# Modulation rows in column tiles of TensorE: four tiles for the early rows, two for the late ones, with the late bias on VectorE

## The chip, the cores and the metric

The kernel runs on one core of one Trainium2 chip. A core has TensorE (PE, which multiplies matrices; its weight loads are listed as PEld), VectorE (DVE), ScalarE (ACT), GpSimd (POOL) and SyncE (SP, which here only issues transfers). TensorE writes its results into PSUM banks of 128 partitions by 512 fp32 values. The metric is the device time of one execution in microseconds (us), lower is better. Everything is fp32, and each fp32 multiplication shows in the trace as two passes (two MATMUL records, each with a weight load).

## The reference

One layer of a diffusion backbone on 128 context tokens and 1024 latent tokens with 1024 channels. What matters here is its beginning:

```
mod = silu(cvec) @ ada_w + ada_b                # 1024 -> 6144, for c_ctx and for c
sh1, sc1, gt1, sh2, sc2, gt2 = split(mod, 6)
h = rms_norm(x, norm1) * (1 + sc1) + sh1
p = h @ w_in                                    # 1024 -> 2432
... token mixing (scans and pooling), output projection with gt1,
... a mixture of 16 experts with sh2, sc2, gt2, final norm
```

The modulation has two rows of 6144 values, one for the context's vector `c_ctx`, one for the latent's `c`. `sh1` and `sc1` (the first 2048 columns) are needed before the projection `h @ w_in` can begin; the other 4096 are needed only after the token mixing.

## The kernel before

The phases run one after the other: projection (`project_phase`, 0 to about 407 us), scans, output projection, experts, final norm. The change touches `project_phase` only, and the parameter table that the host packs.

**Orders.** Each engine has its own program, written out by hand in the function under `@block.<engine>`; semaphores order them (`wait_ge`). The order of work within an engine is therefore fixed, and a waiting instruction holds all that stand behind it.

**Modulation.** The 6144 columns are made in 12 rows of 512 columns (`NADA`), each for both vectors. A row of `ada_w` (1024 x 512, 2 MB) comes in two halves of 1 MB into `ada`, a buffer that holds one row. SyncE's `load_ada(j)` issues half `h` once the semaphore `ada_used` says that the same half of row j-1 has been used, and then the bias `ada_b` (2 KB, on one partition).

- *Early rows*, j = 0 to 3 (`NEARLY` = 4): TensorE's `modulate(j)` multiplies, for each of the eight groups of 128 channels, `silu_c` (128 x 2) with the 128 x 512 weights, all into partitions 0 and 1 of `ps_row`, and adds the bias by a multiplication with `ones` on one partition (L512, L514). ScalarE's `take_row` copies the 2 x 512 result to `mod_row` (L329). TensorE's `turn_row` transposes it in four pieces into `ps_mod` (L530). After row 3, VectorE copies `ps_mod` to `mod` (L439) and derives `g1`.
- *Late rows*, i = 0 to 7: VectorE's `modulate(i)` (L485, L487) multiplies and adds the weights by the channels' factors, sixteen operations of 128 x 512 for each row (eight for each vector), into `mod_sum`. TensorE's `add_up(i)` then adds up the 128 partitions with `pick_row` and adds the bias (L523, L524). ScalarE takes the row and sends it to memory (`modrow`).

**Tokens.** x arrives in three groups of three tiles of 128 tokens. ScalarE squares them (L334), VectorE scales them (L434), TensorE transposes them (`turn_x`, L539), and ScalarE copies the result to `hT` (`take_x`, L347). TensorE's order in the early part is: `turn_x(0)`, `modulate(0)`, `turn_x(1)`, `turn_x(2)`, `turn_row(0)`, then `modulate(j)` and `turn_row(j)` for j = 1 to 3. ScalarE's is: all squares, `take_x(0)`, `take_row(0)`, `take_x(1)`, `take_x(2)`, then the rows 1 to 3. When `mod` is there, ScalarE (L373) and VectorE (L447) apply the modulation to `hT`.

**Projection.** 19 projections of 128 output columns (`project(n, b)`, L563: 24 fp32 multiplications, 48 passes with 384 moving columns), in pairs: `pair(i)` is two projections and then `add_up(i - 1)`. Their weights `win` (0.5 MB each) have two buffers. ScalarE copies each result from PSUM to `pad`. The first four projections feed GpSimd's pooling, the other fifteen VectorE's `shift` (L453 to L467). VectorE's loop is: `modulate(i + 1)`, then two shifts. After the pairs come the pooling's four multiplications (L587) and the last projection.

Of the kernel before, what the change touches and what calls it, by code (L numbers as in the profile page):

```python
# [17 lines left out]
ALU = mybir.AluOpType  # L18
ACT = mybir.ActivationFunctionType
# [36 lines left out]
for _name, _k in (("c", 16), ("norm1", 8), ("mu", NZ), ("pool_scale", 4), ("head", 4 * 10)):  # L56
    PCOLS[_name] = (_n, _n + _k)
    _n += _k
# [61 lines left out]
def project_phase(nc, st, io, keep):  # L120
# [6 lines left out]
    ones = cst[0:1, CCOLS["blk"][0]:CCOLS["blk"][0] + 2]  # L127

    hT = keep["wide"][:].rearrange("p (k c) -> p k c", k=KT)
    HK = KT // 2  # L130
    ada = sb("ada", [P, 2, HK, 512])
    ada_b = sb("ada_bias", [1, 512])
    mod_row = sb("mod_row", [2, 512])

    mod_sum = sb("mod_sum", [P, 2, 512])
    pick_row = sb("pick_row", [P, 2, 2])
# [9 lines left out]
    silu_c = sb("silu_c", [P, KT, 2])  # L146
# [73 lines left out]
    def _(eng):  # L220
        def load_ada(j):
            for h in range(2):
                if not isinstance(j, int) or j > 0:
                    eng.wait_ge(ada_used, 2 * j - 1 + h)
                eng.dma_start(ada[:, h], ada_v[h, :, :, ds(j * 512, 512)]).then_inc(ada_in[h], 16)
            if not isinstance(j, int) or j > NEARLY:

                eng.wait_ge(row_ps, j - NEARLY)
            eng.dma_start(ada_b[:], io["ada_b"][ds(j * 512, 512)].unsqueeze(0)).then_inc(ada_in[1], 16)
# [19 lines left out]
        for n in range(2, 4):  # L249
            eng.wait_ge(win_used, n - 1)  # L250
            load_win(n)
        load_ada(NEARLY)
        eng.dma_start(pw[:], io["pool_w"].rearrange("g c d -> c g d")).then_inc(pw_in, 16)

        eng.wait_ge(zero_set, 1)
# [18 lines left out]
    def _(eng):  # L274
# [4 lines left out]
        for s in range(2):  # L279
            for r in range(2):  # L280
                eng.memset(pick_row[:, s, r:r + 1], float(r == s)).then_inc(pick_set, 1)
# [41 lines left out]
    def _(eng):  # L323
        def take_row(j, late=False):
# [4 lines left out]
            eng.activation(mod_row[:], ps_row[0:2], ACT.Copy).then_inc(row_sb, 1)  # L329
# [56 lines left out]
        def pair(i):  # L386
# [9 lines left out]
            eng.dma_start(io["modrow"][:, ds((i - 1) * 512, 512)], mod_row[:]).then_inc(row_out, 16)  # L396
# [22 lines left out]
    def _(eng):  # L419
        ch = Chain(eng, pre_chain)  # L420
        eng.wait_ge(silu_done, 1)
        ch(eng.tensor_tensor(silu_c[:].rearrange("p k s -> p (k s)"), sig_c[:], par[:, 0:16], ALU.mult))
# [3 lines left out]
        for g in range(3):  # L426
# [45 lines left out]
        def modulate(i):  # L472
# [5 lines left out]
            for h in range(2):  # L478
                eng.wait_ge(ada_in[h], (i + NEARLY + 1) * 16 * (h + 1))
# [24 lines left out]
    def _(eng):  # L504
        def modulate(j):

            for h in range(2):
                eng.wait_ge(ada_in[h], 16 * (h + 1) * (j + 1))
# [2044 lines left out]
```

## Time and profile before

| | us |
|---|---|
| median of 3 runs | 3016.3 (3009.99 to 3019.97) |
| the profiled execution | 3018.82 |
| its span, first to last instruction | 3016.4 |
| TensorE busy in the span | 2721.9 (90%) |
| VectorE busy | 1158.6 (38%) |
| ScalarE busy | 577.9 (19%) |
| GpSimd busy | 564.9 (19%) |
| mean granted TensorE clock | 0.956 of full |

The busy times are sums over stages with different limits, so the table alone does not say what an edit in one stage is worth. Times in the rows below count from the start of the span. The granted clock is given as a share of 2.4 GHz; it has two levels in this trace, 1.00 and 0.50, and a figure between is a mean over a stretch.

### The profile page before, as it was taken

The page shows a single profiled execution, that of the slowest core. Times are in us where ns is not written, and L with a number is a line of the kernel's source. Part 1 is how long each engine was busy: PE and PEld are TensorE (multiplying, and loading weights), DVE is VectorE, ACT ScalarE, POOL GpSimd, SP SyncE. Part 2 cuts the span into 40 slices and gives each one's busy share as a digit, 9 for nine tenths or more (in the row PEclk, how much of TensorE's full clock was granted, in tenths as well). Part 3 has the DMA queues.
Part 4 walks back from the last instruction along what each step waited for, and adds up shares of the span by engine and source line. Part 5 has one row for each costly group of instructions (what it writes and reads, how often), then busy time and mean ns, then how long its engine had stood idle before and what let it go on. Part 6 is the DMA issues. An engine that isn't in the chain of part 4 may idle for free. (4 is left out here: it accounts for less than half of the span.)

```text
span 3016.4 us, 75964 instructions
## 1 busy us (share of the span) xinstructions
PE 2721.9 (90%) x33244; PEld 2404.6 (80%) x33244; DVE 1158.6 (38%) x3005; ACT 577.9 (19%) x1471; POOL 564.9 (19%) x571
## 2 busy tenths in 40 slices
PE   7999958887878897967999999999999999999991
PEld 2555527787877883437999999999999999999991
DVE  1388565555564443334213321232223221332125
ACT  4010153343442332320000100011000100010002
POOL 0683024434445331000000000000000000000002
PEclk9999978898999999978999999999999999999996
DMA  5522210000001004017687777777687768777753
GB/s 206 166 98 84 84 40 7 3 4 7 4 6 38 6 5 179 28 50 294 258 315 266 266 265 275 280 282 271 242 317 281 269 243 316 266 266 264 276 210 133
DMA packets 235260, 517.97 MB, mean 172 GB/s; under 512 B 9854, under 2 KB 42878, under 8 KB 234939
## 3 DMA queue, kind: packets, MB, share of 16 engines
q1 hardware_dynamic: 224410, 483.14, 43.8%
q0 software_dynamic: 8176, 21.83, 3.0%
q10 hardware_dynamic: 2480, 10.06, 0.8%
q8 instruction: 166, 2.72, 0.4%
q14 instruction: 28, 0.22, 0.0%
HBM read 488.68 MB, written 26.33 MB: 171 GB/s over the span
## 5 line engine op out<-in xcount | busy, mean ns | idle before, releaser
L2313 PE MATMUL ps_h<-xT,w1c 128*128 128x144 f32 x4096 | 547.3, 287 | 1.3 <-ACT xT L2119 1.3
L2313 PE MATMUL ps_h<-xT,w3c 128*128 128x144 f32 x4096 | 544.4, 287 | 0.0
L2313 PEld LDWEIGHTS ps_h<-xT,w1c 128*128 128x128 f32 x4096 | 520.5, 191 | 1.7 <-ACT xT L2119 1.7
L2313 PEld LDWEIGHTS ps_h<-xT,w3c 128*128 128x128 f32 x4096 | 519.9, 191 | 0.0
L2323 PE MATMUL ps_ye<-he,w2c 128*128 128x144 f32 x4096 | 512.3, 286 | 0.0
L2323 PEld LDWEIGHTS ps_ye<-he,w2c 128*128 128x128 f32 x4096 | 505.9, 191 | 0.0
L2268 DVE TENSOR_TENSOR u<-ps_h,sig 128x144 f32<-128x144 f32 x256 | 78.7, 307 | 888.7 <-ACT sig L2150 888.7
L563 PE MATMUL front_bank<-wide,win 128*128 128x384 f32 x912 | 298.1, 489 | 2.0 <-DVE wide L447 2.0
L2150 ACT ACTIVATE sig<-ps_h 128x144 f32<-128x144 f32 x256 | 74.3, 290 | 1065.9 <-PE ps_h L2313 1065.9
L563 PEld LDWEIGHTS front_bank<-wide,win 128*128 128x128 f32 x912 | 173.8, 191 | 127.3 <-issue 9.2
L2181 POOL DMA_INDIRECT acc<-ys,idx_s x16 | 25.8, 1615 | 1002.8 <-ACT ye_p L2139 872.0
L896 POOL TENSOR_TENSOR lm<-am,cst 128x256 f32<-128x256 f32 x216 | 162.4, 768 | 231.4 <-DVE am L1269 88.4
L1280 DVE TENSOR_TENSOR tw<-bank,tw 128x512 f32<-128x512 f32 x144 | 99.1, 690 | 260.9 <-PE bank L1438 260.8
L1438 PE MATMUL bank<-tw,xw 64*64 64x64 f32 x2880 | 170.8, 223 | 11.0 <-issue 9.5
L1438 PE MATMUL bank<-xw,tw 64*64 64x64 f32 x2304 | 151.7, 226 | 21.7 <-ACT xw L1064 16.3
L1438 PEld LDWEIGHTS bank<-tw,xw 64*64 64x64 f32 x2880 | 154.0, 139 | 18.2 <-issue 14.2
L1438 PEld LDWEIGHTS bank<-xw,tw 64*64 64x64 f32 x2304 | 135.0, 141 | 28.1 <-ACT xw L1064 19.9
L2175 POOL DMA_INDIRECT xs<-h,idx_s x17 | 17.0, 1001 | 706.0 <-DVE idx_p L2238 706.0
L1438 PE MATMUL bank<-tw,lm 64*64 64x64 f32 x2880 | 112.8, 224 | 24.5 <-POOL lm L896 13.7
L1438 PEld LDWEIGHTS bank<-tw,lm 64*64 64x64 f32 x2880 | 104.3, 139 | 31.0 <-issue 16.0
L2219 DVE TENSOR_SCALAR_CACHE_REDUCE after<-prow,pcol 128x128 f32<-128x128 f32 (+2 forms) x153 | 115.5, 755 | 0.1
L487 DVE SCALAR_TENSOR_TENSOR mod_sum<-ada,silu_c,mod_sum 128x512 f32<-128x512 f32 x112 | 104.9, 936 | 5.5 <-DVE mod_sum L487 1.6
(284 smaller groups left out, 3146.1 us busy)
## 6 DMA issues: line engine op xcount, KB each, us to landing
w1c<-in_w SPq DMA_DIRECT2D x64, 2048.0 KB, 8.0
w3c<-in_w SPq DMA_DIRECT2D x64, 2048.0 KB, 13.0
w2c<-in_w SPq DMA_DIRECT2D x64, 2048.0 KB, 13.2
ada<-in_ada_w SPq DMA_DIRECT2D x24, 1024.0 KB, 6.1
prow<-probsT ACTq DMA_DIRECT2D x17, 576.0 KB, 7.1
win<-in_w_in SPq DMA_DIRECT2D x19, 512.0 KB, 3.9
z<-in_x_all SPq DMA_DIRECT2D x3, 1536.0 KB, 13.9
acc<-zero SPq DMA_DIRECT2D x9, 512.0 KB, 7.0
```

What stands on the lines that cost most here:

```text
L487: mc(eng.scalar_tensor_tensor(out, ada[:, h, k], c, out, ALU.mult, ALU.add))
L563: ins = eng.matmul(ps_p[b][c][:, 0:PIECE], win[:, b, k], hT[:, k, c * PIECE:(c + 1) * PIECE], start=(k == 0), stop=(k == KT - 1))
L896: eng.tensor_tensor(lm[:, b, lv % 2].rearrange("p (d h) c -> p d h c", d=2), am[:, n % 4, :, :, 2], lvl[:, :, lv].unsqueeze(2).to_broadcas ...
L1280: ins = eng.tensor_tensor(flat, INV[b][:], flat, ALU.add)
L1438: return eng.matmul(out, a, b, start=start, stop=stop, skip_group_check=True)
L2150: eng.activation(sig[:, f % 2], ps_h[f % 2][:, 0:SLOTS], ACT.Sigmoid).then_inc(sig_done, 1)
L2175: eng.indirect_dma_start(xs[:], None, io["h2"], bass.IndirectOffsetOnAxis(ap=idx_s[:, 0], axis=0)).then_inc(gathered, 16)
L2181: eng.indirect_dma_start(io["acc"], bass.IndirectOffsetOnAxis(ap=idx_s[:, 1], axis=0), ys[:], None, compute_op=ALU.add).then_inc(scattered ...
L2219: eng.tensor_scalar(after[:, 0:hi - me], prow[:, me:hi], p, None, ALU.is_gt, ALU.add, accum_out=cnts[:, t, 1:2])
L2268: eng.tensor_tensor(u[:, f % 2], ps_h[f % 2][:, 0:SLOTS], sig[:, f % 2], ALU.mult).then_inc(u_done, 1)
L2313: ins = eng.matmul(ps_h[g % 2][:, off:off + SLOTS], w[:, b, k, f * P:(f + 1) * P], xT[:, k], start=(k == 0), stop=(k == KT - 1))
L2323: ins = eng.matmul(yps(k), w2c[:, b, f, k * P:(k + 1) * P], he[:, b, f], start=(c == 0 and f == 0 and k % 3 == 0), stop=(c == NCHUNK - 1 a ...
```

## The change

1. `modulate` on TensorE sends the four channel groups of each half to four column tiles: group k writes the partitions 32k to 32k + 31 of `ps_row`. For this `silu_c` is widened from 2 to 32 columns, of which 30 are zero. Groups k and k + 4 are added in the same tile, and four partial sums stand in four groups of partitions. The bias is no longer added here.
2. `take_row` copies all 128 partitions for an early row, 33 for a late one.
3. `turn_row` multiplies `mod_row` (128 x 128 pieces) with `pick` (128 x 2, ones where a partition holds the wanted vector) in place of the four transposes. This turns the row and adds the four partial sums. `pick` is made by VectorE in three additions from the identity matrix.
4. The early bias comes with the parameter table (`ada_b`, 16 columns), and is added in VectorE's operation that takes `ps_mod` to `mod`.
5. Late rows: `add_up` multiplies `ones` (128 x 1) with `mod_sum` of each vector, in two column tiles (partitions 0 and 32), with no bias. The bias row stands on partition 0 of `ada_b`, whose other partitions are zero, and is added in the first of VectorE's operations for each vector, which becomes a scalar_tensor_tensor in place of a tensor_scalar.
6. `load_ada` loads no bias for early rows; for late rows it issues the bias ahead of the first half, after the wait for `ada_used` and with no wait for `row_ps`.

```diff
@@ load_ada (SyncE)
                 if not isinstance(j, int) or j > 0:
                     eng.wait_ge(ada_used, 2 * j - 1 + h)
+                if h == 0 and (not isinstance(j, int) or j >= NEARLY):
+
+                    eng.dma_start(ada_b[0:1], io["ada_b"][ds(j * 512, 512)].unsqueeze(0)).then_inc(ada_in[0], 16)
                 eng.dma_start(ada[:, h], ada_v[h, :, :, ds(j * 512, 512)]).then_inc(ada_in[h], 16)
-            if not isinstance(j, int) or j > NEARLY:
-
-                eng.wait_ge(row_ps, j - NEARLY)
-            eng.dma_start(ada_b[:], io["ada_b"][ds(j * 512, 512)].unsqueeze(0)).then_inc(ada_in[1], 16)
@@ take_row (ScalarE)
-            eng.activation(mod_row[:], ps_row[0:2], ACT.Copy).then_inc(row_sb, 1)
+            rows = slice(0, CG + 1) if late else slice(0, P)
+            eng.activation(mod_row[rows], ps_row[rows], ACT.Copy).then_inc(row_sb, 1)
@@ VectorE
-        ch(eng.tensor_tensor(silu_c[:].rearrange("p k s -> p (k s)"), sig_c[:], par[:, 0:16], ALU.mult))
+        ch(eng.memset(silu_c[:], 0.0))
+        ch(eng.tensor_tensor(silu_c[:, :, 0:2], sig_c[:].rearrange("p (k s) -> p k s", s=2),
+                             par[:, 0:16].rearrange("p (k s) -> p k s", s=2), ALU.mult))
...
+            if g == 0:
+                eng.wait_ge(const_in, 16)
+                ch(eng.tensor_tensor(pick[:], ident[:, 0:2], ident[:, CG:CG + 2], ALU.add))
+                for q in range(2, 4):
+                    ch(eng.tensor_tensor(pick[:], pick[:], ident[:, q * CG:q * CG + 2], ALU.add))
...
-        ch(eng.tensor_copy(mod[:], ps_mod[:, 0:4 * KT].rearrange("p (e s) -> p e s", s=2)))
+        b0, b1 = PCOLS["ada_b"]
+        ch(eng.tensor_tensor(mod[:], ps_mod[:, 0:4 * KT].rearrange("p (e s) -> p e s", s=2),
+                             par[:, b0:b1].unsqueeze(2).to_broadcast([P, 2 * KT, 2]), ALU.add))
@@ modulate (VectorE, late rows)
-                            mc(eng.tensor_scalar(out, ada[:, h, k], c, None, ALU.mult))
+                            mc(eng.scalar_tensor_tensor(out, ada[:, h, k], c, ada_b[:], ALU.mult, ALU.add))
@@ modulate (TensorE, early rows)
-                    ins = eng.matmul(ps_row[0:2], silu_c[:, h * HK + k], ada[:, h, k], start=(h == 0 and k == 0), stop=False)
-                if h == 1:
-                    ins = eng.matmul(ps_row[0:2], ones, ada_b[:], start=False, stop=True)
+                    ins = eng.matmul(ps_row[k * CG:(k + 1) * CG], silu_c[:, h * HK + k], ada[:, h, k], start=h == 0, stop=h == 1,
+                                     skip_group_check=True)
                 ins.then_inc(ada_used, 1)
@@ add_up (TensorE, late rows)
             for s in range(2):
-                eng.matmul(ps_row[0:2], pick_row[:, s], mod_sum[:, s], start=(s == 0), stop=False)
-            eng.matmul(ps_row[0:2], ones, ada_b[:], start=False, stop=True).then_inc(row_ps, 1)
+                ins = eng.matmul(ps_row[s * CG:s * CG + 1], ones[:], mod_sum[:, s], start=True, stop=True)
+            ins.then_inc(row_ps, 1)
@@ turn_row (TensorE)
             eng.wait_ge(row_sb, j + 1)
+            if j == 0:
+                eng.wait_ge(pre_chain, 5 + 2)
             for q in range(4):
                 e = 4 * j + q
-                ins = eng.transpose(ps_mod[:, 2 * e:2 * e + 2], mod_row[:, q * P:(q + 1) * P], ident[0:2, 0:2])
+                ins = eng.matmul(ps_mod[:, 2 * e:2 * e + 2], mod_row[:, q * P:(q + 1) * P], pick[:], start=True, stop=True)
```

(`CG` is 32. The rest of the diff changes buffer sizes, semaphore counts and the packing of the parameters.)

## Rows read from the trace of the kernel before

**Rows 1.** stage windows: busy per engine, granted clock, DMA share, GB/s
```profile
0.00:69.00 69.00, 49.01 (x160) 18.91 (x160) 9.44 (x24) 25.29 (x48) 3.43 (x13) 0.93 0.63 225
69.00:407.00 338.00, 329.18 (x984) 180.97 (x984) 213.14 (x232) 45.76 (x107) 141.50 (x137) 0.99 0.31 103
404.00:470.00 66.00, 30.36 (x529) 19.40 (x531) 43.95 (x59) 31.05 (x60) 33.77 (x26) 0.59 0.04 10
...
1400.00:2960.00 1560.00, 1554.41 (x12742) 1553.80 (x12740) 409.06 (x1625) 139.29 (x413) 80.85 (x63) 1.00 0.75 270
```

**Rows 2.** timeline of TensorE, early part: start, duration, instruction, idle before
```profile
18.85 7.03 PE L512 MATMUL front_bank<-ada,silu_c 128*2 128x512 f32 x16
...
28.82 7.10 PE L539 MATMUL front_bank<-cst,z 128*128 128x128 f32 x48 [1.99 <-DVE z L434]
35.85 0.41 PE L530 MATMUL front_bank<-cst,mod_row 2*128 2x2 f32 x4
36.18 7.03 PE L512 MATMUL front_bank<-ada,silu_c 128*2 128x512 f32 x16
43.14 1.02 PE L514 MATMUL front_bank<-ada_bias,cst 1*2 1x512 f32 x2
...
66.70 0.41 PE L530 MATMUL front_bank<-cst,mod_row 2*128 2x2 f32 x4 [0.73 <-ACT mod_row L329]
69.11 61.27 PE L563 MATMUL front_bank<-wide,win 128*128 128x384 f32 x184 [2.01 <-DVE wide L447]
```

**Rows 3.** timeline of ScalarE, early part
```profile
27.61 3.02 ACT L347 ACTIVATE wide<-front_bank 128x512 f32<-128x512 f32 x6
...
44.25 0.59 ACT L329 ACTIVATE mod_row<-front_bank 2x512 f32<-2x512 f32 x1 [6.88 <-PE front_bank L514]
```

**Rows 4.** timeline of SyncE's DMA issues, early part
```profile
39.81 4.75 SPq L225 DMA_DIRECT2D ada<-in_ada_w  x2
```

**Rows 5.** DMA issues, 39 to 44 us: size, us to landing
```profile
ada<-in_ada_w SPq DMA_DIRECT2D x1, 1024.0 KB, 5.1
```

**Rows 6.** DMA totals, 15 to 23 us: packets and mean rate
```profile
DMA packets 887, 3.27 MB, mean 409 GB/s; under 512 B 33, under 2 KB 33, under 8 KB 887
```

**Rows 7.** windows after idle stretches of TensorE, columns as above
```profile
46.10:49.40 3.30, 3.30 (x5) 0.51 (x4) 0.00 (x0) 0.00 (x0) 0.00 (x0) 0.50 1.02 370
...
237.30:240.50 3.20, 3.20 (x4) 0.26 (x2) 2.95 (x2) 0.00 (x0) 3.12 (x2) 0.50 1.07 393
```

**Rows 8.** TensorE group: 128 stationary columns, two moving
```profile
L2284 PE MATMUL ps_i<-pick,hot 128*128 128x2 f32 x272 | 33.1, 253 | 26.6 <-DVE hot L2229 26.6
```

**Rows 9.** TensorE timeline in the scan stage: 64x64 tiles, two by two
```profile
584.53 1.10 PE L1438 MATMUL bank<-wide 64*64 64x128 f32 x32
```

**Rows 10.** weight loads of the same 64x64 tiles, groups by form
```profile
L1438 PEld LDWEIGHTS bank<-wide 64*64 64x64 f32 x32 | 0.9, 133 | 0.0
```

**Rows 11.** timeline of TensorE, projection stage
```profile
132.90 1.88 PE L523 MATMUL front_bank<-mod_sum,pick_row 128*2 128x512 f32 x4
...
135.65 31.23 PE L563 MATMUL front_bank<-wide,win 128*128 128x384 f32 x96
...
237.16 3.57 PE L523 MATMUL front_bank<-mod_sum,pick_row 128*2 128x512 f32 x4 [2.46 <-DVE mod_sum L487]
```

**Rows 12.** timeline of VectorE, projection stage
```profile
168.27 2.43 DVE L453 TENSOR_TENSOR nsum<-pad 128x1153 f32<-128x1153 f32 x1 [3.78 <-ACT pad L384]
...
177.18 1.30 DVE L485 TENSOR_SCALAR mod_sum<-ada,silu_c 128x512 f32<-128x512 f32 x2 [0.65 <-DVE z L467]
178.51 8.73 DVE L487 SCALAR_TENSOR_TENSOR mod_sum<-ada,silu_c,mod_sum 128x512 f32<-128x512 f32 x6
...
210.05 2.60 DVE L485 TENSOR_SCALAR mod_sum<-ada,silu_c 128x512 f32<-128x512 f32 x2 [0.62 <-DVE z L467]
212.69 11.09 DVE L487 SCALAR_TENSOR_TENSOR mod_sum<-ada,silu_c,mod_sum 128x512 f32<-128x512 f32 x6
...
258.52 4.69 DVE L487 SCALAR_TENSOR_TENSOR mod_sum<-ada,silu_c,mod_sum 128x512 f32<-128x512 f32 x6
```

More of the change, by code:

```diff
@@ L55 @@
 _n = 0
-for _name, _k in (("c", 16), ("norm1", 8), ("mu", NZ), ("pool_scale", 4), ("head", 4 * 10)):
+for _name, _k in (("c", 16), ("norm1", 8), ("mu", NZ), ("pool_scale", 4), ("ada_b", 16), ("head", 4 * 10)):
     PCOLS[_name] = (_n, _n + _k)
@@ L125, in project_phase @@
     ident = cst[:, 0:P]
-    ones = cst[0:1, CCOLS["blk"][0]:CCOLS["blk"][0] + 2]
     hT = keep["wide"][:].rearrange("p (k c) -> p k c", k=KT)
     HK = KT // 2
+    CG = P // 4
     ada = sb("ada", [P, 2, HK, 512])
-    ada_b = sb("ada_bias", [1, 512])
-    mod_row = sb("mod_row", [2, 512])
+    ada_b = sb("ada_bias", [P, 512])
+    mod_row = sb("mod_row", [P, 512])
     mod_sum = sb("mod_sum", [P, 2, 512])
-    pick_row = sb("pick_row", [P, 2, 2])
+    pick = sb("front_pick", [P, 2])
+    ones = sb("front_ones", [P, 1])
     mod = sb("mod", [P, 2 * KT, 2])
@@ L145, in project_phase @@
     nsum = sb("nsum", [P, NTOK + 1])
-    silu_c = sb("silu_c", [P, KT, 2])
+    silu_c = sb("silu_c", [P, KT, CG])
     sig_c = sb("sig_c", [P, 16])
@@ L251, in _ @@
             load_win(n)
+        eng.wait_ge(zero_set, 2)
         load_ada(NEARLY)
         eng.dma_start(pw[:], io["pool_w"].rearrange("g c d -> c g d")).then_inc(pw_in, 16)
-        eng.wait_ge(zero_set, 1)
         for t in range(NT):
@@ L278, in _ @@
         eng.memset(zero[:], 0.0).then_inc(zero_set, 1)
-        for s in range(2):
-            for r in range(2):
-                eng.memset(pick_row[:, s, r:r + 1], float(r == s)).then_inc(pick_set, 1)
+        eng.memset(ada_b[:], 0.0).then_inc(zero_set, 1)
+        eng.memset(ones[:], 1.0).then_inc(pick_set, 1)
         eng.memset(pad[:], 0.0).then_inc(pad_zero, 1)
@@ L395, in pair @@
             eng.wait_ge(row_sb, i + NEARLY)
-            eng.dma_start(io["modrow"][:, ds((i - 1) * 512, 512)], mod_row[:]).then_inc(row_out, 16)
+            eng.dma_start(io["modrow"][:, ds((i - 1) * 512, 512)], mod_row[0:2 * CG:CG]).then_inc(row_out, 16)
         eng.wait_ge(pad_zero, 1)
@@ L507, in modulate @@
             for h in range(2):
-                eng.wait_ge(ada_in[h], 16 * (h + 1) * (j + 1))
+                eng.wait_ge(ada_in[h], 16 * (j + 1))
                 if h == 0 and j > 0:
@@ L544, in _ @@
         turn_x(0)
-        eng.wait_ge(pre_chain, 1)
+        eng.wait_ge(pre_chain, 2)
         modulate(0)
@@ L574, in _ @@
             project(n, n)
-        eng.wait_ge(pick_set, 4)
+        eng.wait_ge(pick_set, 1)
         pair(1)
@@ L2524 @@
     par[:, 1:16:2] = cols(a["c"][0])
-    for name, v in (("norm1", a["norm1"][0]), ("mu", a["mu_shift"][0]), ("pool_scale", a["pool_scale"][0])):
+    for name, v in (("norm1", a["norm1"][0]), ("mu", a["mu_shift"][0]), ("pool_scale", a["pool_scale"][0]),
+                    ("ada_b", a["ada_b"][0][:2 * D])):
         par[:, PCOLS[name][0]:PCOLS[name][1]] = cols(v)
```

2 lines of the change are left out of this document (1 added, 1 removed).

## The prediction

> **What bounds the kernel now.** I read the stage windows first [rows 1]: for each stretch they give the busy time of each engine and the granted clock. TensorE is busy in 1554.4 of 1560 us of the expert stage (1400 to 2960 us), which the change does not touch. The change lives in the first 407 us. There, two stretches behave differently.
>
> In the early part (0 to 69 us) TensorE works 49 us and the DMA engines 63% of the time. The timeline of TensorE [rows 2] shows a chain of four modulation rows. Each row is sixteen passes (eight fp32 multiplications of two passes, 7.03 us), two bias passes (1.02 us), a copy by ScalarE, and four transposes (0.41 us). The first projection starts at 69.11 us, after the last turn (66.70) and VectorE's and ScalarE's scaling. SyncE loads a half of the next row's weights only when the matching half has been used: the first issue for row 2 stands at 39.81 [rows 4], 3.63 us after row 1 began at 36.18.
>
> From 69 to 407 us TensorE is busy 329 of 338 us at clock 0.99 [rows 1], so a saving there counts, unless another engine is close behind. VectorE is: at 237.16 TensorE had waited 2.46 us for `mod_sum`, and its next four passes took 3.57 instead of 1.88 us [rows 11], at clock 0.50, i.e. 1.2 GHz [rows 7]. After 407 us nothing is edited; I let the whole rest move with the end of the projections.
>
> **Do column tiles run side by side?** No row shows four tiles on the same 128 partitions. The nearest are the scan's 64x64 tiles, two by two: 32 passes with 128 moving columns in 1.10 us [rows 9]. A pass in the full array with 384 columns takes 31.23/96 = 0.325 us [rows 11], so 128 columns are 0.108 us and 32 in line would be 3.5 us; they ran four at a time, and in each four two column tiles share their rows. So two side by side is shown for `add_up`; for the early rows I take four (nearest row: four in flight at once), with bounds two and one. One pass of 512 columns is 7.03/16 = 0.43 us at full clock, 0.85 at half.
>
> The Trainium skill ("TensorE: Matmul & The Clock Gate", Part 3, The mechanism) says that a weight load overlaps a running matmul only when the row group differs, which speaks against this change, as all its column tiles share one row group. The trace leans against that: the 32 weight loads of those tiles took 133 ns each, 4.3 us in line, and all lay inside the 0.9 us [rows 10]. By the rule the result would be no gain; it is a rival below.
>
> **Early part, step by step.** Row 0 becomes four slots of 0.43 us instead of 8 us, but buys nothing: what comes next, the transposes of the second token group, starts at 28.82 only because ScalarE first empties the first group's banks, from 27.61 on [rows 2, 3]; its copies wait behind its squares, and those for the arrival of x. The row shows VectorE as releaser, whose work was long done. So 35.85 stands unchanged, where the first row is turned.
>
> The turn: four transposes (0.33 us until the next row starts [rows 2]) become four fp32 multiplications, eight passes with 128 stationary and 2 moving columns. These cost 33.1/272 = 0.12 us each [rows 8], so 1.0 us, +0.65. Row 1 starts at 36.85. Its first half is two slots, about 0.9 us plus 0.2 for the pipeline's end, so SyncE issues row 2's first half at 37.95 instead of 39.81, its second at 38.8. A lone 1 MB half takes 5.1 us to land [rows 5], and a second behind it another 2.6 (1.05 MB at 409 GB/s [rows 6]): 43.05 and 45.65. Now the row waits for data, not the data for the row. Removing the bias load saves SyncE 0.36 us of issue, hidden.
>
> The two projection weights of 0.5 MB, issued behind row 2, keep the queue busy to 48.3 (another 2.6). Row 3's halves, issued when row 2's are used (about 45 and 47.6), therefore land at 50.9 and 53.5; I take 51.2 and 53.8, since these loads come in small pieces. TensorE idles between halves, and idle of this size was followed by clock 0.50 already [rows 7]; so I take half clock: 1.7 us for the last half, 0.2 for the end: 55.7. Copy and hand-over to TensorE took 44.89 - 44.25 = 0.64 us [rows 2, 3] (the copy's time goes by its 512 columns, not its partitions): 56.35. The turn at half clock is 8 x 0.24 = 1.95: 58.3. From the start of the turn to projection was 2.41 us [rows 2], 2.0 without the transposes' 0.41: 60.3. The bias on VectorE changes a copy of 32 elements into an addition of 32, and the extra memset and the three small `pick` operations lie in VectorE's idle time before 24 us: nothing, and some 0.5 us altogether if that cover were gone. Gain 69.11 - 60.3 = 8.8 us, less 0.5 as the first projection, whose first multiplications are paced by the scaling anyway, runs longer at half clock: **8.3 us**. Bounds: at full clock throughout the chain ends about 1.9 us sooner (10.7); with two tiles only it is 3.8 us later (4.5).
>
> **Late part.** An `add_up` costs 135.65 - 132.90 = 2.75 us now [rows 11]: six passes of 0.43 and 0.17 for the changes of shape. Now it is two pairs side by side, 0.95 us: 1.8 less, eight times, 14.4 us if TensorE were the bound throughout.
>
> It is not between 168 and 257 us. VectorE's chain from 168.27 (released by ScalarE's copy of a projection, [rows 12]) to 237.16 has no wait over 0.7 us in it; the one before it was 3.78 us. After the change it starts 1.8 us sooner, by the first `add_up`'s saving. But the two operations that open each row turn from tensor_scalar into scalar_tensor_tensor. While GpSimd pools, these took 1.30/2 = 0.65 against 8.73/6 = 1.46 us in the row at 177, and 2.60/2 = 1.30 against 11.09/6 = 1.85 in the one at 210 [rows 12]: +1.6 and +1.1. With 0.25 us of a wait that vanishes, this `add_up` starts 1.8 - 2.7 + 0.25 = -0.65, later than before, measured from the projections' start; the three gains before it are lost in the wait, which grows from 2.46 to about 8.5 us. That longer idle makes the half clock last longer: before it cost 3.57 - 1.88 = 1.7 us, I add 0.8. The next row ends on VectorE about 1.4 us before TensorE wants it; from there TensorE is the bound (VectorE's passes fall to 0.78 us, 4.69/6 [rows 12]), and five savings count: 5 x 1.8 = 9.0. **Late gain 9.0 - 0.65 - 0.8 = 7.6 us.** Bounds: the opening operations at no extra cost, no extra half clock: 11.1; VectorE late by the same again, with the next row late too: 3.5. The bias load of a late row goes ahead of its first half, waits for the same use, and no longer holds SyncE until `add_up` has run; a 2 KB load, hidden by a row period of 34 us. `row_out`'s rows 0 and 32 instead of 0 and 1 cost nothing while ScalarE is busy 46 of 338 us [rows 1].
>
> **Sum.** 8.3 + 7.6 = 15.9 us. The profiled execution took 3018.8 us (span 3016.4 and 2.4 around it), so 3002.9; it lies 2.5 above the median of the runs, from which the forecast is 3016.3 - 15.9 = **3000.5 us**, 0.5% faster.
>
> **Rivals.** (1) VectorE swallows the late gain to its bound: 8.3 + 3.5 = 11.8, 3004.5 us. For it: 26 us for one row while pooling. Against: at 258 us its passes are back at 0.78 us [rows 12], so GpSimd's pooling no longer holds it. (2) Only two tiles run side by side: 4.5 + 7.6 = 12.1, 3004 us. (3) None do; the change doesn't do what it says. Early 3 x (1.1 - 0.6) - 0.6 = 0.9; late an `add_up` saves 0.95, but the start of the fourth is 0.95 - 2.7 + 0.25 = -1.5, so 5 x 0.95 - 1.5 = 3.3: 3012 us. (4) Each weight load waits as well: +16 x 0.133 us for three rows, 6.4, and 5 x 4 x 0.133 = 2.7 late, so 4.2 - 9.1: 3021 us. That is the case of the skill's rule, and the loads in [rows 10] speak against it. (5) The other side: the scan stage starts at another moment, and the granted clock falls for longer. From 404 to 470 us it averages 0.59 [rows 1], about 54 us at half. One more such stretch, with 30 of 66 us of TensorE work done at half speed by then costing up to 27 us, would give 3016.3 - 15.9 + 27 = 3027 us; it makes the kernel slower by 0.3% from about 25 us lost, some 50 us of half clock. Nothing in the edit calls for it.
>
> **How the numbers follow.** The forecast has 0.66, rival (1) 0.12, (2) 0.08, (3) 0.06, (4) 0.04, (5) 0.04. A difference under 0.3% (9 us) is about what the measurement can't tell from none. The forecast, (1) and (2) lie beyond it, by so little that I give part of them to no change: faster 0.78, same 0.18, slower 0.04. The likeliest case alone spans 2995 to 3006; the range 2991 to 3011 adds the upper bounds of both parts (10.7 + 11.1 and a little scatter) and reaches near (3).
>
> **What would show it.** Right: sixteen passes of a row within about 2 us at full clock (3.6 at half); row 2's first half issued near 38 us; projection start at 59 to 61.5; `add_up` near 1 us; a wait of 6 to 10 us before the fourth, after which seven periods shrink by 1.8. Wrong: rows of 7 us; projection start above 65; `add_up` waits also at the fifth and later ones; or a scan stage whose length differs from 743 us by more than 5.

## The result and the profile after

The changed kernel takes 3002.1 us in the median of 20 runs (2994.3 to 3006.9), the kernel before 3014.5 (3009.6 to 3020.9, also 20). The ratio is 0.9959, with a 95% interval of 0.9951 to 0.9967: 12.4 us or 0.41% faster. The forecast was 15.9 us less, or 3000.5 us.

The profiled execution of the changed kernel has a span of 2997.8 us, 18.6 less than that of before. That pair flatters the change: the profiled execution of before (3018.8 us) lies 4.3 above the median of its kernel, that of the change (3000.4) 1.7 below its own. By stages it is 7.0 us less up to the first projection, 4.8 from there to the end of the pairs, 7.2 in the scan stage, where nothing was edited, and -0.4 in the rest. The first two, 11.8 us, are about what the 20 runs show. The 7.2 are hardly a gain: 6.0 of the profiles' difference are explained by where the two executions lie, and the last part of the experiments shows how far this stage scatters.

The early part, from the timeline of TensorE in the changed kernel (it answers to [rows 2]; a row is now "128*32", and its halves stand apart where the second waited):

```profile
17.89 1.92 PE L520 MATMUL front_bank<-ada,silu_c 128*32 128x512 f32 x16
29.07 7.76 PE L548 MATMUL front_bank<-cst,z 128*128 128x128 f32 x48 [9.26 <-DVE z L435]
36.67 0.95 PE L539 MATMUL front_bank<-front_pick,mod_row 128*128 128x2 f32 x8
37.55 1.92 PE L520 MATMUL front_bank<-ada,silu_c 128*32 128x512 f32 x16
40.25 1.05 PE L539 MATMUL front_bank<-front_pick,mod_row 128*128 128x2 f32 x8 [0.78 <-ACT mod_row L328]
43.82 1.73 PE L520 MATMUL front_bank<-ada,silu_c 128*32 128x512 f32 x8 [2.52 <-DMA ada<-in_ada_w]
46.57 1.94 PE L520 MATMUL front_bank<-ada,silu_c 128*32 128x512 f32 x8 [1.02 <-DMA ada<-in_ada_w]
49.28 1.87 PE L539 MATMUL front_bank<-front_pick,mod_row 128*128 128x2 f32 x8 [0.78 <-ACT mod_row L328]
52.87 1.93 PE L520 MATMUL front_bank<-ada,silu_c 128*32 128x512 f32 x8 [1.71 <-DMA ada<-in_ada_w]
55.52 1.94 PE L520 MATMUL front_bank<-ada,silu_c 128*32 128x512 f32 x8 [0.72 <-DMA ada<-in_ada_w]
58.23 1.87 PE L539 MATMUL front_bank<-front_pick,mod_row 128*128 128x2 f32 x8 [0.78 <-ACT mod_row L328]
62.11 65.07 PE L572 MATMUL front_bank<-wide,win 128*128 128x384 f32 x192 [2.01 <-DVE wide L455]
```

Sixteen passes take 1.92 us at full clock where they took 7.03: four column tiles run side by side. But from row 2 on TensorE waits for each half (`<-DMA`), and the last two rows take as long as the transfers do. At 43.82 and 46.57 the eight passes of a half take 1.7 to 1.9 us, where half of a row at full clock is about 1.0: the clock. These are windows of the changed kernel (columns as in [rows 1], they answer to [rows 7]):

```profile
23.70:33.70 10.00, 4.63 (x22) 4.66 (x23) 4.85 (x10) 8.97 (x19) 0.00 (x0) 0.50 0.54 198
44.20:67.90 23.70, 16.68 (x57) 7.37 (x50) 4.55 (x11) 7.37 (x10) 0.00 (x0) 0.50 0.48 158
228.50:238.50 10.00, 5.96 (x11) 2.44 (x12) 9.34 (x7) 0.59 (x1) 9.50 (x8) 0.50 0.47 159
```

The granted clock is 0.50, i.e. 1.2 GHz, for 10 us around the second group of transposes, for 24 us from row 2 into the first projections, and for 10 us around the fourth `add_up`. Before each of these TensorE had less to do, or stood idle. SyncE's issues (they answer to [rows 4]):

```profile
38.67 1.23 SPq L228 DMA_DIRECT2D ada<-in_ada_w  x2
39.94 2.98 SPq L232 DMA_DIRECT2D win<-in_w_in  x2
45.59 3.35 SPq L228 DMA_DIRECT2D ada<-in_ada_w  x2
```

Row 2's loads went out from 38.67, then the two projection weights, then row 3's from 45.59.

The late part, TensorE again (it answers to [rows 11]):

```profile
127.11 1.03 PE L530 MATMUL front_bank<-mod_sum,front_ones 128*1 128x512 f32 x4
...
232.53 1.87 PE L530 MATMUL front_bank<-mod_sum,front_ones 128*1 128x512 f32 x4 [9.01 <-DVE mod_sum L495]
234.34 33.35 PE L572 MATMUL front_bank<-wide,win 128*128 128x384 f32 x96
...
363.96 1.03 PE L530 MATMUL front_bank<-mod_sum,front_ones 128*1 128x512 f32 x4
365.44 8.02 PE L596 MATMUL front_bank<-zpool,pw 128*128 128x384 f32 x24 [0.45 <-ACT pad L383]
```

An `add_up` goes from one projection to the next in 0.96 us (127.11 to 128.07 and so on) instead of 2.75. The fourth, at 232.53, waited 9.01 us for VectorE. Measured from the start of the projections it begins at 170.42 us; before it was 168.05. The projections behind it took 33.35 instead of 31.23 us, at half clock at first. The periods of the others fell from 33.91 to 32.11 us. VectorE in the rows of the third and fourth `add_up` (they answer to [rows 12]):

```profile
170.60 2.71 DVE L493 SCALAR_TENSOR_TENSOR mod_sum<-ada,silu_c,ada_bias 128x512 f32<-128x512 f32 x2 [0.63 <-DVE z L475]
173.35 8.77 DVE L495 SCALAR_TENSOR_TENSOR mod_sum<-ada,silu_c,mod_sum 128x512 f32<-128x512 f32 x6
...
204.91 3.14 DVE L493 SCALAR_TENSOR_TENSOR mod_sum<-ada,silu_c,ada_bias 128x512 f32<-128x512 f32 x2 [0.61 <-DVE z L475]
208.08 11.09 DVE L495 SCALAR_TENSOR_TENSOR mod_sum<-ada,silu_c,mod_sum 128x512 f32<-128x512 f32 x6
```

The two opening operations of a row cost 2.71 and 3.14 us, 1.30 and 2.60 before, 1.95 more in all; the others of these rows are as they were (8.77 and 11.09 for six). The second shift ahead of the third row, which runs beside the pooling, takes 1.0 us longer than before (9.9 us from its start to the row's, 8.9 before).

### The profile page after: what moved, and what is told of

Its sections match the earlier page's. It is cut to its first block and busy times, and to the rows that moved or that the text cites. A ratio compares the mean times of both kernels' runs of the same rounds, so it can differ in the third digit from the quotient of the medians.

```text
span 2997.8 us, 75942 instructions
## 1 busy us (share of the span) xinstructions
PE 2688.1 (90%) x33236; PEld 2400.6 (80%) x33236; DVE 1165.6 (39%) x3009; ACT 577.1 (19%) x1471; POOL 567.0 (19%) x569
```

## The experiments

All edits are to the changed kernel unless said otherwise. "Start" is the first multiplication of the projections in the profile, "scans" the first of the scan stage (69.1 and 408.9 before, 62.1 and 397.1 in the changed kernel). Ratios are to the kernel before, measured beside each run. Most readings of a stage below rest on one profile for each kernel.

**Each part alone.** `e1_early_only` has the early rows of the change with the late rows of before:

```diff
-            rows = slice(0, CG + 1) if late else slice(0, P)
+            rows = slice(0, 2) if late else slice(0, P)
...
-                            mc(eng.scalar_tensor_tensor(out, ada[:, h, k], c, ada_b[:], ALU.mult, ALU.add))
+                            mc(eng.tensor_scalar(out, ada[:, h, k], c, None, ALU.mult))
...
-                ins = eng.matmul(ps_row[s * CG:s * CG + 1], ones[:], mod_sum[:, s], start=True, stop=True)
-            ins.then_inc(row_ps, 1)
+                eng.matmul(ps_row[0:2], pick_row[:, s], mod_sum[:, s], start=(s == 0), stop=False)
+            eng.matmul(ps_row[0:2], ones, ada_b[:], start=False, stop=True).then_inc(row_ps, 1)
```

> The early rows of the change alone: four column tiles, bias from the parameter table; the late rows as before. My reading of the two traces: the early part gives 69.1 - 62.1 = 7.0 us by the start of the first projection, and nothing else of the change is in this kernel, so the time is 7 us under before (ratio 0.9977), the wait before the fourth add_up stays near 2.5 us. Rival (the changed kernel's profiled scan stage was 7 us shorter, and the edit causes that): the earlier start shortens the scans too, 14 us under before (0.9954).

Measured: ratio 0.9971 (0.996 to 0.9981), 8.7 us; start 62.65, scans 400.4. The scan stage took 750.2 us (before 749.3): it did not become shorter. The fourth `add_up`:

```profile
230.33 1.88 PE L533 MATMUL front_bank<-mod_sum,pick_row 128*2 128x512 f32 x4 [2.31 <-DVE mod_sum L498]
```

It waited 2.31 us, about as before (2.46), but stayed at full clock: 1.88 us, where before it took 3.57. So the clock behind such a wait differs from profile to profile, and the 4.8 us between start and scans hold some of that: from start to scans this kernel, whose late rows are those of before, took 337.7 us, 2.1 less than before.

`e2_late_only` is the kernel before with the late rows of the change, and with 32 stationary columns instead of 2 in the early ones (the edit is shown against the kernel before):

```diff
-                eng.matmul(ps_row[0:2], pick_row[:, s], mod_sum[:, s], start=(s == 0), stop=False)
-            eng.matmul(ps_row[0:2], ones, ada_b[:], start=False, stop=True).then_inc(row_ps, 1)
+                ins = eng.matmul(ps_row[s * CG:s * CG + 1], ones[:], mod_sum[:, s], start=True, stop=True)
+            ins.then_inc(row_ps, 1)
...
-                            mc(eng.tensor_scalar(out, ada[:, h, k], c, None, ALU.mult))
+                            mc(eng.scalar_tensor_tensor(out, ada[:, h, k], c, ada_b[:], ALU.mult, ALU.add))
```

> The late rows of the change alone: add_up in two column tiles, bias on VectorE; early rows as before in one tile with their bias on TensorE (the stationary operand padded to 32 columns). My reading: projections start at 69 us, add_up costs about 0.95 us instead of 2.75, the fourth add_up waits 8 to 9 us for VectorE, and from the start of the projections to the end of the pairs 4.8 to 6 us are gained (6 if the slower first projection of the changed kernel comes from its half clock): ratio 0.998 to 0.9984. Rival (TensorE is the bound all along): eight savings of 1.8 us, 14 us, ratio 0.9952. Together with the early part alone it should add up to the 12 us of the whole change.

Measured: ratio 0.9984 (0.9972 to 0.9996), 4.8 us. Start and the fourth `add_up`, and behind them row 2 of the kernel before:

```profile
67.11 63.85 PE L568 MATMUL front_bank<-wide,win 128*128 128x384 f32 x192 [2.01 <-DVE wide L452]
...
236.35 1.87 PE L528 MATMUL front_bank<-mod_sum,front_ones 128*1 128x512 f32 x4 [9.05 <-DVE mod_sum L492]
```

```profile
45.23 8.72 PE L512 MATMUL front_bank<-ada,silu_c 128*2 128x512 f32 x16
```

The start is 2.0 us sooner than before, though the early rows are not in tiles. Rows 2 and 3 took two times 3.62 us here, 8.72 and 8.69 before, where half clock fell into both; up to the start this profile has 3.4 us of half clock, that of before 10.2. `e4_one_tile` below, also with 32 columns in one tile, has 3.4 too; whether the columns do that or chance was not tested. Against this start the early rows of the change are worth 5.0 us, not 7.0.

The wait is 9.05 us, as in the whole change. From start to scans it took 333.4 us; before 339.8, the whole change 335.0. The two parts multiply to 0.9955; the whole is 0.9959. So the gains add up within what these intervals can tell (each is over 6 us wide), and eight full savings (0.9952 for this part alone) lie outside. The late rows are worth 4.8 us by this kernel, and about 3.6 by the whole change less `e1_early_only`.

**How many tiles run side by side.** In `e3_two_tiles` and `e4_one_tile` the number n of column tiles of the early rows is 2 and 1, and 64 and 32 partitions are copied and turned:

```diff
-ps_row[k * CG:(k + 1) * CG], ..., start=h == 0, stop=h == 1
+ps_row[(k % n) * CG:(k % n + 1) * CG], ..., start=(h == 0 and k < n), stop=(h == 1 and k >= HK - n)
```

> The changed kernel with its early rows in two column tiles instead of four (64 partitions copied and turned). If four tiles really run side by side in the change and two here, a row takes 3.4 us at full clock, and the projections start 2 to 3 us later than 62.1, at 64 to 65. If only two ran side by side before, nothing moves: 62.1.

> The changed kernel with its early rows in one column tile (32 partitions copied and turned, the bias still from the parameter table). If the gain of the early part is the tiles' and is cut short by the arrival of the weights, a row takes 6.9 us again and the projections start at 66 to 67 us, i.e. the tiles are worth 4 to 5 us, not the 3 x 5.2 = 15.5 us by which three rows are shorter. If the gain is that of the bias passes (1.1 us a row), the start stays near 62 to 63.

A row and the start with two tiles:

```profile
37.31 3.63 PE L520 MATMUL front_bank<-ada,silu_c 128*32 128x512 f32 x16
...
64.73 5.85 PE L572 MATMUL front_bank<-wide,win 128*128 128x384 f32 x9 [2.01 <-DVE wide L455]
```

and with one:

```profile
37.23 7.05 PE L520 MATMUL front_bank<-ada,silu_c 128*32 128x512 f32 x16
...
55.90 7.05 PE L520 MATMUL front_bank<-ada,silu_c 128*32 128x512 f32 x16 [0.83 <-DMA ada<-in_ada_w]
...
66.75 3.86 PE L572 MATMUL front_bank<-wide,win 128*128 128x384 f32 x7 [2.01 <-DVE wide L455]
```

At full clock sixteen passes take 7.05, 3.63 and 1.92 us with one, two and four tiles, so each tile counts. The starts are 66.75, 64.73 and 62.11: three rows shorter by 15.4 us together bring 4.6. With one tile the row waits 0.83 us for data in all; with four the data are the bound. And the one-tile kernel keeps its clock better (3.4 us at half up to the start, 28.3 in the change): it reaches its first `add_up` 63.8 us after the start, the four-tile kernel after 65.0. Net of that, four tiles are worth 3.4 us over one. Each was run once (3006.1 and 3006.5 us), which cannot tell them from the change; the profiles can.

**What bounds the early part now.** `e6_win_last` moves the projection weights behind row 3:

```diff
-            if j == 2:
+            if j == 3:
                 for n in range(2):
                     load_win(n)
```

> The changed kernel with the first two projection weights loaded behind row 3 instead of row 2. If row 3's weights arrive late because 1 MB stands ahead of them in the queue, its halves land near 50.7 and 53.4 instead of 52.8 and 55.5, and the projections start about 2 us sooner, near 60. Rival: SyncE's issue (it waits for the use of row 2) sets the arrival, and nothing moves.

```profile
50.36 1.94 PE L520 MATMUL front_bank<-ada,silu_c 128*32 128x512 f32 x8
53.22 1.94 PE L520 MATMUL front_bank<-ada,silu_c 128*32 128x512 f32 x8 [0.92 <-DMA ada<-in_ada_w]
...
59.82 10.44 PE L572 MATMUL front_bank<-wide,win 128*128 128x384 f32 x27 [2.02 <-DVE wide L455]
```

Row 3's first half is there when TensorE comes (no wait at 50.36; 52.87 in the changed kernel), and the start moves by 2.3 us to 59.82. Not all of that is the edit's: in this profile the turn of row 2, which the edit cannot reach, already stands at 48.56 instead of 49.28. Net of these 0.7 us it is worth 1.6. The queue ahead of row 3 was the cause, not SyncE's issue. (One run, 3001.9 us.)

`e8_keep_warm` fills TensorE's waits with multiplications whose result nobody reads:

```diff
+        def spin(out, n, cols=384):
+            for _ in range(n):
+                eng.matmul(out[:, 0:cols], ident, cst[:, P:P + cols], start=True, stop=True)
...
         modulate(0)
+        spin(ps_mod, 12)
         turn_x(1)
...
+            if j == 1:
+                eng.wait_ge(x_stored, NT)
+            spin(banks[0], 2 if j == 2 else 3)
```

(and one more before a second half and before a turn, for j over 1).

> The changed kernel with idle multiplications of the identity on TensorE in the waits of the early part (into banks whose content is no longer or not yet wanted): its clock should stay at full. My reading of the early part: half clock costs 0.8 us in the transposes, about 0.9 in the last half of row 3, 0.9 in its turn, so the projections start 2 to 2.5 us sooner (59.6 to 60), and the first add_up comes at 63.8 from their start instead of 65.0: 3 to 4 us in all. Rival: the multiplications themselves stand in the way of the rows, and the start is at 62 or later.

```profile
55.08 1.59 PE L526 MATMUL front_bank<-ada,silu_c 128*32 128x512 f32 x8
...
57.45 1.05 PE L545 MATMUL front_bank<-front_pick,mod_row 128*128 128x2 f32 x8
...
60.52 9.75 PE L584 MATMUL front_bank<-wide,win 128*128 128x384 f32 x28
...
226.29 1.87 PE L536 MATMUL front_bank<-mod_sum,front_ones 128*1 128x512 f32 x4 [6.79 <-DVE mod_sum L495]
```

The half clock up to the start falls from 28.3 to 3.4 us; the last turn takes 1.05 us (1.87 in the changed kernel), the start is at 60.52, the first `add_up` 62.6 us after it. Together that is 4.0 us, the upper end of the expectation. The fourth `add_up` surprised: it waits 6.79 us instead of 9.01, 103.2 us after the first (105.4 in the changed kernel), though nothing was edited there. VectorE's operations fell differently beside GpSimd's pooling, for example 1.36 us for the first shift's opening operation between the third row and the fourth, where the changed kernel has 2.20. (One run, 3000.8 us, with a scan stage of 751.2 us.)

`e10_warm_win` has both edits:

> The changed kernel with the idle multiplications in the early part and the projection weights loaded behind row 3. Each alone brought the end of the pairs 4.3 (loads) and 7.3 us (clock) forward in the one profile. If both causes of the early part's loss are real and separate, the projections start near 58 us and scans start at 388 us instead of 397: 8 to 9 us under the changed kernel, about 2993 to 2994 us, ratio 0.9935. Rival: these are the luck of one profile (the scan stage differed by up to 10 us between profiles), then the ratio stays at 0.996.

```profile
51.52 1.07 PE L526 MATMUL front_bank<-ada,silu_c 128*32 128x512 f32 x8 [0.42 <-DMA ada<-in_ada_w]
...
56.42 62.63 PE L584 MATMUL front_bank<-wide,win 128*128 128x384 f32 x192
...
224.45 1.87 PE L536 MATMUL front_bank<-mod_sum,front_ones 128*1 128x512 f32 x4 [9.06 <-DVE mod_sum L495]
```

Ratio 0.9926 (0.9912 to 0.994), 22 us under before and clear of the change alone. Start 56.42, scans 388.9. So the two causes together are real; the share of each rests on the profiles: the start is 3.4 us sooner than with the moved weights alone and 4.1 than with the clock kept alone. The fourth `add_up` waits 9.06 us, and the 2.3 us that `e8_keep_warm` had gained there are gone.

**What VectorE's opening operations cost.** `e7_no_late_bias` gives VectorE back its tensor_scalar, with no bias, so its output lacks that bias:

```diff
-mc(eng.scalar_tensor_tensor(out, ada[:, h, k], c, ada_b[:], ALU.mult, ALU.add))
+mc(eng.tensor_scalar(out, ada[:, h, k], c, None, ALU.mult))
```

> The changed kernel with the bias of the late rows left out: VectorE's two opening operations are tensor_scalar again (the output lacks that bias). If those operations are what made the fourth add_up later, it starts 2 to 2.7 us sooner from the start of the projections (168 instead of 170.4), the wait before it is near 6.5 us instead of 9. Rival: the later row comes from another overlap with GpSimd's pooling; then it stays at 170.

```profile
228.25 1.87 PE L530 MATMUL front_bank<-mod_sum,front_ones 128*1 128x512 f32 x4 [5.16 <-DVE mod_sum L495]
```

The wait is 5.16 us, and the fourth `add_up` comes 166.5 us after the start instead of 170.4: 3.9 us, more than the 2 to 2.7 expected, and the pairs end 5.4 us sooner. The edit gains, but not by those operations alone: they took 2.17 and 2.33 us in the third and fourth row, against 2.71 and 3.14, which is 1.35 together. The rest lies in operations that were not edited and fell differently beside the pooling, as they had in `e8_keep_warm` without this edit. From the first `add_up` to the fourth it took 101.6 us here, 105.4 in the change and 103.2 in e8, so by these profiles the opening operations are worth somewhere between 1.6 and 3.9 us. (One run, 2996.5 us.)

**Can the wait be ordered away?** `e5_addup_later` moves each `add_up` behind the next projection:

```diff
         def pair(i):
-            for b in range(2):
-                project(2 * i + b, b)
-            add_up(i - 1)
+            project(2 * i, 0)
+            if not isinstance(i, int) or i > 1:
+                add_up(i - 2)
+            project(2 * i + 1, 1)
```

> The changed kernel with each add_up moved behind the first projection of the next pair (15.6 us later in TensorE's order), and ScalarE's taking of the row moved with it. If the late gain was lost because TensorE waits 9 us for VectorE's row and then works at half clock, both go: no wait of TensorE on mod_sum, no half clock near 230 us, and from the start of the projections to the end of the pairs some 11 us less (about 292 instead of 303): 2991 us, ratio to before 0.992. Rival: VectorE is the bound in these pairs whatever the order, so the wait moves to the copies and shifts of a projection (TensorE waits for ScalarE, ScalarE for pad), and nothing is gained.

Ratio 0.9958 (0.9944 to 0.9971). The fourth `add_up`, then VectorE's opening operations in the projection stage (a group: busy, mean ns, idle before it by releaser):

```profile
242.91 1.87 PE L537 MATMUL front_bank<-mod_sum,front_ones 128*1 128x512 f32 x4 [3.65 <-DVE mod_sum L502]
```

```profile
L500 DVE SCALAR_TENSOR_TENSOR mod_sum<-ada,silu_c,ada_bias 128x512 f32<-128x512 f32 x16 | 14.9, 932 | 37.3 <-PE front_bank L537 28.9 <-DMA ada<-in_ada_w 5.7 <-DVE z L482 2.5
```

The wait fell to 3.65 us, not to nothing. VectorE now waits 28.9 us in all for the `add_up` that frees the single `mod_sum`, which I had not seen. That this keeps the 3.65 us alive is argued; the next experiment did not bear it out. The scans start 5.0 us sooner in the profile, but the runs do not separate it from the change: inconclusive as a gain.

`e9_later_between` then reorders VectorE's loop to go with it:

```diff
-            modulate(i + 1)
-            for b in range(2):
-                shift(2 * i + b, b, Chain(eng, shift_chain, (2 * i + b) * PER))
+            shift(2 * i, 0, Chain(eng, shift_chain, 2 * i * PER))
+            modulate(i + 1)
+            shift(2 * i + 1, 1, Chain(eng, shift_chain, (2 * i + 1) * PER))
```

> As the kernel with each add_up one projection later, and VectorE's loop reordered to shift, modulate, shift (there modulate stood first and waited for the later add_up to free mod_sum). If the single mod_sum is what kept a wait of 3.7 us and the half clock alive, the wait of TensorE on VectorE goes, the clock holds, and the pairs end about 292 to 293 us after the start of the projections (303.3 in the changed kernel, 297.5 with add_up moved alone): 2991 to 2993 us, ratio 0.992. Rival: VectorE's load under GpSimd's pooling is too high for any order; then TensorE waits elsewhere and the pairs end at 297 again.

VectorE, and then four of the eight `add_up`s:

```profile
144.26 1.38 DVE L468 TENSOR_TENSOR nsum<-pad 128x1153 f32<-128x1153 f32 x1 [14.43 <-ACT pad L383]
```

```profile
177.69 1.87 PE L537 MATMUL front_bank<-mod_sum,front_ones 128*1 128x512 f32 x4 [2.70 <-DVE mod_sum L502]
...
214.56 1.42 PE L537 MATMUL front_bank<-mod_sum,front_ones 128*1 128x512 f32 x4 [3.15 <-DVE mod_sum L502]
...
254.47 1.87 PE L537 MATMUL front_bank<-mod_sum,front_ones 128*1 128x512 f32 x4 [6.07 <-DVE mod_sum L502]
...
372.90 1.87 PE L537 MATMUL front_bank<-mod_sum,front_ones 128*1 128x512 f32 x4 [2.99 <-DVE mod_sum L502]
```

A miss: ratio 0.998 (0.9969 to 0.999), slower than the change. VectorE stands idle for 14.4 us before 144.26, waiting for a projection, and is then late for four of the eight rows, the last one too. `e11_all` puts this order on `e10_warm_win`:

> All three at once: later add_up with VectorE's loop reordered, idle multiplications in the early part, projection weights behind row 3. If the three causes add up: scans start near 380 us, 27 us sooner than before the change and 17 sooner than after it, 2985 to 2987 us, ratio 0.990 to 0.991. Rival: the clock part and the late part overlap (the half clock at the fourth add_up is counted in both), then 384 to 385.

Ratio 0.9958 (0.9943 to 0.9973), scans 399.4: the early edits gain, the order gives it back. Neither of the two cases expected.

**The bias back on TensorE, in tiles.** `e12_bias_tiles` is `e10_warm_win` with:

```diff
             for s in range(2):
-                ins = eng.matmul(ps_row[s * CG:s * CG + 1], ones[:], mod_sum[:, s], start=True, stop=True)
+                eng.matmul(ps_row[s * CG:s * CG + 1], ones[:], ada_b[:], start=True, stop=False, skip_group_check=True)
+            for s in range(2):
+                ins = eng.matmul(ps_row[s * CG:s * CG + 1], ones[:], mod_sum[:, s], start=False, stop=True, skip_group_check=True)
...
-                            mc(eng.scalar_tensor_tensor(out, ada[:, h, k], c, ada_b[:], ALU.mult, ALU.add))
+                            mc(eng.tensor_scalar(out, ada[:, h, k], c, None, ALU.mult))
```

> The kernel with idle multiplications and the projection weights behind row 3, and the late bias moved from VectorE back to TensorE, but in the two column tiles (ones times the padded bias row, then ones times mod_sum; VectorE opens each row with tensor_scalar again, and the bias is loaded behind the second half once add_up has run, as before the change). An add_up then takes 0.86 us more, 1.8 in all. My reading: the fourth add_up starts 3 to 4 us sooner from the start of the projections (164 to 165 instead of 168.0), since VectorE is the bound up to there; the four add_ups after it cost 0.86 us each, 3.4, and the fourth itself 0.9. So the end of the pairs stays within 1 us of the kernel without this edit (300.3 from the start of the projections), ratio to before 0.9925. Rival: the tensor_scalar gains nothing where the bias load waits for add_up; then it is 4 us slower, 0.994.

TensorE at the fourth and fifth `add_up`, then VectorE in the row that the third waits for:

```profile
220.39 1.03 PE L537 MATMUL front_bank<-ada_bias,front_ones 128*1 128x512 f32 x4 [2.19 <-DVE mod_sum L496]
221.25 1.03 PE L539 MATMUL front_bank<-mod_sum,front_ones 128*1 128x512 f32 x4
...
253.86 1.03 PE L537 MATMUL front_bank<-ada_bias,front_ones 128*1 128x512 f32 x4 [0.42 <-DVE mod_sum L496]
```

```profile
162.01 2.17 DVE L494 TENSOR_SCALAR mod_sum<-ada,silu_c 128x512 f32<-128x512 f32 x2 [0.65 <-DVE z L476]
164.22 7.58 DVE L496 SCALAR_TENSOR_TENSOR mod_sum<-ada,silu_c,mod_sum 128x512 f32<-128x512 f32 x6
```

Ratio 0.9907 (0.989 to 0.9923), 28 us: the fastest of all in the median, though its interval overlaps that of `e10_warm_win`. The fourth `add_up` starts 163.7 us after the start of the projections (168.0 in e10), the wait is 2.19 us, and the clock holds through it: half clock from the start to the scans falls from 15.2 to 3.4 us. That last item I had left out; it gives back 2.8 us (0.8 in the `add_up`, 2.0 in the projections behind it) of the 4.3 that five `add_up`s now cost more at 0.86 each. The scans start at 386.2, 2.6 us sooner than in `e10_warm_win`. That is no more than the alignment with the pooling moves by itself: e8, with the change's late rows, took 329.3 us from start to scans, this kernel 329.6. So the gain of this edit is not shown apart.

**The scan stage.** Its length in the fourteen profiles (first 64x64 multiplication to the first of the output projection), with no edit in it:

| kernel | us | kernel | us |
|---|---|---|---|
| before | 749.3 | e6_win_last | 746.4 |
| change | 742.1 | e7_no_late_bias | 746.4 |
| e1_early_only | 750.2 | e8_keep_warm | 751.2 |
| e2_late_only | 750.7 | e9_later_between | 744.6 |
| e3_two_tiles | 747.3 | e10_warm_win | 748.7 |
| e4_one_tile | 744.2 | e11_all | 744.8 |
| e5_addup_later | 740.7 | e12_bias_tiles | 740.3 |

It scatters over 11 us and does not go with the edits: e1 and e2, the two halves of the change, have the lengths of before. So nothing here makes the 7.2 us of the change's profile a gain. There is one profile for each kernel, so what differs between kernels and what between executions cannot be told apart here. Half clock alone does not set it either: before has 108 us of it in this stage at 749.3, e12 112 at 740.3. What sets the length stays open.

## Why the prediction was right, point by point

The sign and the mechanism were right; the size was too large: 12.4 us were measured, 15.9 forecast. That 3002.1 us lies only 1.6 from the forecast 3000.5 is partly luck: the median of before was taken from three runs as 3016.3 and is 3014.5 over twenty, 1.8 of the 3.5 us by which the gain was too high. The terms:

- **Four tiles side by side: right.** 1.92 us for sixteen passes; e3 and e4 show that two and one take 3.63 and 7.05. The row it rested on was weaker than said: 32 passes in 1.10 us, where 3.46 stand in line, are 3.1 at a time, not four. The weight-load rule of the Trainium skill ("TensorE: Matmul & The Clock Gate", Part 3, The mechanism), my rival (4), does not hold here: by it a row would have stayed at 7 us or more.
- **The early part becomes bound by the weights: right**, shown by e4 (15.4 us of shorter rows are worth 4.6) and e6 (1.6 us by what stands ahead in the queue).
- **Start at 60.3: off by 1.8 us** (62.1), and outside the 59 to 61.5 named as a sign of being right. "35.85 stands unchanged" failed first: row 0's brevity leaves TensorE idle for 9.26 us, the transposes behind it start 0.25 later and take 7.76 instead of 7.10, partly at half clock, and the first turn stands at 36.67, 0.8 late. Row 2's issue (38.67 instead of 37.95) and its data carry this on. The rest is the queue: I gave the two projection weights 2.6 us; row 3's data came 1.7 us later than I had them, 0.9 of which row 2's already were.
- **0.5 us of the first projections at half clock: too small**, 1.2 (65.0 against 63.8 to the first `add_up`). At full clock throughout it is 62.6 (e8, e10). It varies: e1 and e6, with 24 to 28 us of half clock up to the start as well, took 63.6.
- **`add_up` saves 1.8 us and only five count: right.** e2 excludes the eight. "Seven periods shrink by 1.8" among the signs contradicts this sum: five did, the one behind the fourth shrank by 0.5, and the one before it grew by 4.8.
- **The fourth `add_up` 0.65 later: 2.4 from the start of the projections, 1.2 without the half clock of the first projections.** The mechanism, more work for VectorE beside the pooling, is right, its parts are not. The opening operations cost 1.95 us more in the profile, not 2.7; the shift ahead of them took 1.0 longer, which the sum doesn't have; and the 0.25 us of a wait did not vanish. e7 shows that the opening operations matter, and that their size depends on how VectorE's work falls beside GpSimd's. The wait is 9.0 us, where I had 8.5.
- **0.8 us more of half clock after it: 1.3.** The projections behind it took 33.35 us, 2.1 over the usual. That the `add_up` of before paid 1.7 is itself one profile's: e1's, behind the same wait, paid nothing.
- **Not foreseen:** a wait of 0.45 us for ScalarE's last copy behind the eighth `add_up` (365.44).

The misses are 1.8 + 0.7 + 0.5 + 0.5 + 0.5 = 4.0 us of the 4.1 between 15.9 and the 11.8 of the profile, all of one sign. The clock's part follows from TensorE getting idle; the queue, VectorE and ScalarE make the rest.

Of the rivals, (1), VectorE swallows the late gain, describes the loss best in kind. In total its 11.8 us are nearer to the 12.4 measured than the forecast's 15.9, and so are the 12.1 of (2); the total alone would not have told them apart. The profiles tell more: the fifth `add_up` has no wait, where (1)'s bound has it late; from the first `add_up` to the end of the pairs the profile of the change gave 6.0 us, where (1) has 3.5 (the runs of e1 and e2 put the late rows at 3.6 to 4.8); and part of the loss is in the early rows. (2), (3) and (4) are excluded by the 1.92 us of a row. (5), a longer scan stage, did not come. The last sign of being wrong, a scan stage more than 5 us off 743, compares with windows cut at 407 and 1150 us; measured as in the table, before itself is 749.3, and with 11 us of scatter the sign says nothing.

## What to carry to other kernels

When a short chain of work is made almost four times shorter, price what is idle next: here 70% of the time saved in the rows met the arrival of the weights, and the idle time itself halved TensorE's clock for the work behind it. Look at who shares the port or the buffer with the engine that takes over work: two additions for each row moved to VectorE cost 0.5 us alone (1.54 against 1.01) and 1.6 to 3.9 us over two rows where GpSimd pooled beside them. One profile of such an overlap is not enough to price an edit: without any edit in it, the same stretch moved by 2.2 us. Compare stages, not spans, between two profiles: the unedited stage differed by up to 11 us here, nearly the whole gain.

## What the runs showed of the hardware

- Column tiles run side by side for fp32 on the same 128 rows: sixteen passes with 32 stationary and 512 moving columns take 7.05, 3.63 and 1.92 us in one, two and four tiles. By these three a slot (one pass in each tile) costs 0.43 us, with 0.2 us on top for the whole; four tiles are 3.7 times as fast as one. 32 stationary columns instead of 2 cost nothing that shows (7.05 against 7.03 us).
- Going to column tiles and back costs about 0.1 us (0.96 us for an `add_up` of two slots of 0.43).
- Multiplications whose result is thrown away keep the clock up: half clock before the projections fell from 28.3 us to 3.4 (e8) and to none (e10); with them and the moved load the kernel is 10 us faster than the change, by the ratios (0.9926 against 0.9959).
- The granted clock behind a wait of TensorE at an `add_up` does not follow from the wait's length alone. Waits of 9.0 to 9.3 us (change, e2, e4, e6, e10) went with 10.2 us at half clock, which began within the wait. With shorter ones it was 6.9 us for 8.33 (e3), 6.79 (e8) and 3.65 (e5), but 3.4 for 5.16 (e7); 3.4 for 2.46 (before) and 2.70 (e9), but none for 2.31 (e1), 2.68 (e11) and 2.19 (e12).
